# A long convolution's transforms taken at odd half frequencies, with its matmuls in groups of four banks

## The reference

```python
# hyena: v, x1, x0 are short convolutions (width 3) of the projection
z = v * x1
# h_fwd, h_bwd: 256 taps each, from a small MLP with sine activations times a decay
# y[t] = sum_{s<=t} h_fwd[t-s] z[s] + sum_{s>t} h_bwd[s-t] z[s]   (two-sided, per channel)
y = (longconv(z, h_fwd, h_bwd) + hy_skip * z) * x0
```

## Time and profile before

| | |
|---|---|
| median of three executions | 2644.22 us |
| the profiled execution's own time | 2645.37 us |
| its span, first to last instruction | 2643.6 us |
| granted PE clock, mean | 0.998 |
| PE, DVE, ACT, POOL busy | 2626.3, 1931.1, 1509.1, 387.5 us |
| PE matmuls in float32 of `fkm`, `zfm`, `zim` (records; two make a matmul) | 40, 32, 48 |

### The profile page before, as it was taken

One profiled execution on the slowest core, in us unless ns is written; L12 is line 12 of the kernel. 1 busy time (PEld: TensorE's weight loads), 2 busy tenths in 40 slices (PEclk: granted clock), 3 DMA queues, 4 the chain that ended last, 5 costly groups with the idle time before them and its releaser, 6 DMA issues.

```text
span 2643.6 us, 38894 instructions
## 1 busy us (share of the span) xinstructions
PE 2626.3 (99%) x15146; PEld 2279.0 (86%) x15146; DVE 1931.1 (73%) x2902; ACT 1509.1 (57%) x2345; POOL 387.5 (15%) x383
## 2 busy tenths in 40 slices
PE   9999999999999999999999999999999999999998
PEld 8888888888899888888888888888888888888887
DVE  7877777877967665666666698697877777777775
ACT  6655658786656444444444466545565555555555
POOL 2111003214201010000000052011101010101012
PEclk9999999999999999999999999999999999999999
DMA  7666566666656555666666666546666666666664
GB/s 238 211 190 184 176 199 188 185 197 186 201 173 196 168 159 170 189 191 187 192 188 191 191 190 220 160 128 194 188 191 186 191 190 191 189 191 188 191 184 135
DMA packets 136992, 492.89 MB, mean 186 GB/s; under 512 B 15463, under 2 KB 16552, under 8 KB 136552
## 3 DMA queue, kind: packets, MB, share of 16 engines
q1 hardware_dynamic: 136376, 489.88, 61.5%
q10 hardware_dynamic: 432, 0.52, 0.1%
HBM read 488.21 MB, written 2.13 MB: 185 GB/s over the span
## 4 chain that ended last, share of the span: by engine, by line
PE 97%; DVE 1%; ACT 1%; issue 0%; DMA 0%; SPq 0%; DVEq 0%; ACTq 0%
PE ps L871 61%; PE ps L868 30%; PE ps L885 1%; DVE wl L1443 1%; PE ps L1056 0%; DMA raw<-in_w_sc 0%; PE ps L1089 0%; PE ps L1078 0%; PE ps L1002 0%; ACT wh L1120 0%; PE ps L858 0%; PE ps L857 0%; PE ps L856 0%; PE ps L848 0%; PE ps L846 0%
## 5 line engine op out<-in xcount | busy, mean ns | idle before, releaser
L871 PE MATMUL ps<-X,wh 128*128 128x512 f32 x4848 | 1624.8, 397 | 2.6 <-DVE X L1449 2.4
L1443 DVE TENSOR_TENSOR wl<-raw,wh 128x1024 fp32r<-128x1024 f32 (+1 forms) x905 | 1178.4, 1305 | 460.2 <-ACT wh L1120 459.4
L1120 ACT ACTIVATE wh<-raw 128x1024 fp32r<-128x1024 f32 (+1 forms) x905 | 954.3, 1057 | 650.9 <-PE ps L868 612.8
L868 PE MATMUL ps<-X,wl 128*128 128x256 f32 x4848 | 1217.1, 279 | 0.0
L871 PEld LDWEIGHTS ps<-X,wh 128*128 128x128 f32 x4848 | 888.4, 188 | 196.8 <-issue 9.0
L868 PEld LDWEIGHTS ps<-X,wl 128*128 128x128 f32 x4848 | 879.7, 188 | 29.4
L871 PE MATMUL ps<-XG,wh 128*128 128x512 f32 x2176 | 730.8, 396 | 0.6 <-DVE hT L1443 0.6
L868 PE MATMUL ps<-XG,wl 128*128 128x256 f32 x2176 | 547.5, 278 | 0.0
L871 PEld LDWEIGHTS ps<-XG,wh 128*128 128x128 f32 x2176 | 395.6, 188 | 81.6 <-DVE hT L1443 1.5
L868 PEld LDWEIGHTS ps<-XG,wl 128*128 128x128 f32 x2176 | 398.3, 188 | 17.1
L1905 POOL TENSOR_TENSOR hT<-hT,T 128x256 f32<-128x256 f32 x224 | 188.3, 863 | 1426.7 <-DVE hT L1443 1426.6
(11 more groups left out here) (197 smaller groups left out, 1239.0 us busy)
## 6 DMA issues: line engine op xcount, KB each, us to landing
raw<-in_w_gate SPq DMA_DIRECT2D x176, 512.0 KB, 3.9
raw<-in_w_down SPq DMA_DIRECT2D x176, 512.0 KB, 3.8
raw<-in_w_sc SPq DMA_DIRECT2D x95, 512.0 KB, 4.2
raw<-in_w_up SPq DMA_DIRECT2D x88, 512.0 KB, 3.7
raw<-in_w_val SPq DMA_DIRECT2D x88, 512.0 KB, 3.6
raw<-in_w_zx SPq DMA_DIRECT2D x80, 512.0 KB, 4.1
raw<-in_w_in SPq DMA_DIRECT2D x68, 512.0 KB, 3.8
raw<-in_w_osc SPq DMA_DIRECT2D x32, 512.0 KB, 3.8
```

The lines of the kernel that those rows point to most:

```text
L868: t = e.matmul(bank(c, i)[:, 0:256], wl[:, b0:b0 + 128], X[:, kx * 512:kx * 512 + 256], start=False, stop=sp and kk == c.kn - 1)
L871: e.matmul(bank(c, i)[:, :], wh[:, b0:b0 + 128], X[:, kx * 512:kx * 512 + 512], start=st and kk == 0, stop=False)
L1120: return e.activation(out, in_, ACT.Copy, scale=scale)
L1443: return e.tensor_tensor(out, a, b, op)
```

## The change: what it does

The transform is taken at 256 frequencies (2k+1)/1024 instead of 257 frequencies k/512, and even and odd positions are kept apart. With E and O the sums over even and odd positions, each of the lower 128 frequencies is E+O and its mirror in the upper half E-O up to a sign, so one 128 x 128 cosine block for each of even and odd, and one sine block for each, do. `Fm` and `IF` shrink from 1024 to 512 columns.

- `fkm`: 8 single matmuls of 384 columns in two groups of four (banks 4 to 7). ACT copies the even ones, DVE then makes sum and difference straight from the odd banks (two operations each). No single frequency is left, and no `fk0`.
- `ztm`: the transposes read every second position; two steps instead of four. `zfm`: 8 single matmuls in three steps (2, 4, 2), evacuated as `fkm` is.
- a new piece `zc`: four DVE operations of 384 columns per half, before the way back.
- `zim`: per tile 4 matmuls of 128 columns; the three tiles of a half stand in one step. `zi` writes even and odd positions interleaved, read from two halves of the bank.
- `fhm` stands in two groups of four.
- All z pieces now lie between steps 563 and 582; the filter's between 294 and 309.

```diff
             for n in range(8):
-                put(s + 16 + 2 * n, "fhm", n)
-                put(s + 17 + 2 * n, "fh", n)
-            put(s + 33, "fsum", 0)
-            for n in range(10):
-                put(s + 36 + 2 * n, "fkm", n)
-                put(s + 37 + 2 * n, "fk", n)
-            put(s + 57, "fk0", 0)
+                put(s + 16 + 3 * (n // 4), "fhm", n)
+                put(s + 17 + 3 * (n // 4) + n % 4 // 2, "fh", n)
+            for st in range(2):
+                put(s + 22 + st, "fsum", st)
+            for n in range(8):
+                put(s + 26 + 3 * (n // 4), "fkm", n)
+                put(s + 27 + 3 * (n // 4) + n % 4 // 2, "fk", n)
...
+                put(e + 2 + 2 * (n // 2), "ztm", n)
+                put(e + 3 + 2 * (n // 2), "zt", n)
+            for n, d in enumerate((4, 4, 6, 6, 6, 6, 8, 8)):
+                put(e + d, "zfm", n)
+                put(e + d + (2 if n == 5 else 1), "zf", n)
+            for n, d in enumerate((9, 11, 14, 16)):
+                put(e + d, "zk", n)
+            for hf, d in ((0, 13), (1, 18)):
+                put(e + d, "zc", hf)
                 for i in range(3):
-                    put(b + 8 + i, "zim", 3 * hf + i)
-                    put(b + 9 + i, "zi", 3 * hf + i)
-                b += 12
+                    put(e + d + 1, "zim", 3 * hf + i)
+                    put(e + d + 2 + i // 2, "zi", 3 * hf + i)
...
-                    for st in range(2):
-                        t = e.matmul(b[:, 0:384], Fm[:, 512 * st + 128 * m:512 * st + 128 * m + 128],
-                                     zt[:, 768 * st + 384 * h2:768 * st + 384 * h2 + 384], start=(st == 0), stop=(st == 1))
-                    t.then_inc(zfP, 1)
+                    w.wait_ge(zA, 2 * h2 + 2)
+                    if i < 4 and m > 1:
+                        w.wait_ge(zA, 4)
+                    elif i > 3 and m % 2:
+                        w.wait_ge(zfV, m + 1)
+                    elif i > 3:
+                        w.wait_ge(zfA, m // 2 + 1)
+                    e.matmul(banks[4 + m][:, 0:384], Fm[:, 128 * m:128 * m + 128],
+                             zt[:, 768 * (m % 2) + 384 * h2:768 * (m % 2) + 384 * h2 + 384], start=True, stop=True).then_inc(zfP, 1)
...
                 if piece == "zim":
-                    w.wait_ge(zkV, 8 * h2 + 8)
+                    w.wait_ge(zkV, 12 * h2 + 12)
-                    for m in range(4):
-                        t = e.matmul(b[:, 0:256], zf[:, m, 128 * n:128 * n + 128], IF[:, 256 * m:256 * m + 256],
-                                     start=(m == 0), stop=(m == 3))
+                    for st, parts in ((0, (zf[h2][:, 0, ch], zd(h2, 1)[:, ch])), (1, (zd(h2, 0)[:, ch], zf[h2][:, 2, ch]))):
+                        for q in range(2):
+                            t = e.matmul(b[:, 128 * st:128 * st + 128], parts[q], IF[:, 256 * st + 128 * q:256 * st + 128 * q + 128],
+                                         start=(q == 0), stop=(q == 1))
...
+                if piece == "zf" and i % 2:
+                    h2, m = i // 4, i % 4
+                    z0, z1 = zf[h2][:, m - 1, :], zf[h2][:, m, :]
+                    b = banks[4 + m][:, 0:384]
+                    w.wait_ge(zfP, i + 1)
+                    w.wait_ge(zfA, i // 2 + 1)
+                    tt(z0, z1, b, ALU.add).then_inc(zfV, 1)
...
+                if piece == "zc":
+                    z = zf[i]
+                    w.wait_ge(zkV, 12 * i + 8)
+                    tt(zd(i, 0), z[:, 0, :], z[:, 1, :], ALU.subtract).then_inc(zkV, 1)
+                    tt(z[:, 0, :], z[:, 0, :], z[:, 1, :], ALU.add).then_inc(zkV, 1)
+                    tt(zd(i, 1), z[:, 2, :], z[:, 3, :], ALU.subtract).then_inc(zkV, 1)
+                    tt(z[:, 2, :], z[:, 2, :], z[:, 3, :], ALU.add).then_inc(zkV, 1)
                 if piece == "zi":
-                    stt(zT(i), zT(i), P("hy_skip", i), banks[4 + i % 2][:, 0:256], ALU.mult, ALU.add).then_inc(ziV, 1)
+                    o = zT(i).rearrange("p (s q) -> p s q", q=2)
+                    y = banks[4 + n // 2][:, 256 * (n % 2):256 * (n % 2) + 256].rearrange("p (q s) -> p s q", q=2)
+                    stt(o, o, P("hy_skip", i), y, ALU.mult, ALU.add).then_inc(ziV, 1)
```

More of the change, by code:

```diff
@@ L1048, in tensor @@
                 if piece == "fkm":
-                    m, c = i // 2, i % 2
-                    n0, n = (128 * m, 128) if m < 4 else (256, 1)
+                    c, m = i // 4, i % 4
                     w.wait_ge(fV, 27)
-                    if i > 3:
-                        w.wait_ge(fl, 2 + i - 3)
-                    for st in range(2):
[L1055 to L1058, removed]
+                    if c and m % 2:
+                        w.wait_ge(fV, 28 + m)
+                    elif c:
+                        w.wait_ge(fl, 3 + m // 2)
+                    src = (dec[:, 768 * (m % 2):768 * (m % 2) + 768], hf[:, 1536 * (m % 2):1536 * (m % 2) + 768])[m // 2]
+                    e.matmul(banks[4 + m][:, 0:384], Fm[:, 128 * m:128 * m + 128], src[:, 384 * c:384 * c + 384],
+                             start=True, stop=True).then_inc(fP, 1)
                 if piece == "ztm":
-                    st, c = i // 2, i % 2
-                    b = banks[4 + i % 2]
+                    c, st = i // 2, i % 2
                     w.wait_ge(zm, 3 * c + 3)
                     w.wait_ge(fA, 3)
-                    if i > 1:
-                        w.wait_ge(zA, i - 1)
+                    w.wait_ge(fV, 35)
+                    w.wait_ge(fl, 6)
                     for n in range(3):
-                        t = turn(b[:, 128 * n:128 * n + 128], zT(3 * c + n)[:, 128 * st:128 * st + 128])
+                        t = turn(banks[4 + i][:, 128 * n:128 * n + 128], zT(3 * c + n)[:, st::2])
                     t.then_inc(zP, 1)
@@ L1764, in vector @@
                 if piece == "fsum":
-                    w.wait_ge(fV, 22)
-                    e.memset(hf[0:1, 768:1536], 0.0).then_inc(fV, 1)
-                    for st in range(2):
-                        fw, bw = hf[:, 1536 * st:1536 * st + 768], hf[:, 1536 * st + 768:1536 * st + 1536]
-                        w.wait_ge(fV, 23)
-                        tt(dec[:, 768 * st:768 * st + 768], fw, bw, ALU.add).then_inc(fV, 1)
-                        w.wait_ge(fV, 24 + 2 * st)
-                        tt(fw, fw, bw, ALU.subtract).then_inc(fV, 1)
-                if piece == "fk" and i == 4:
-                    w.wait_ge(fl, 4)
-                    e.tensor_copy(K5[:, 4, :], K5[:, 0, :]).then_inc(fV, 1)
-                if piece == "fk0":
-                    w.wait_ge(fl, 8)
-                    e.memset(K5[0:1, 2, :], 0.0).then_inc(fV, 1)
+                    if i == 0:
+                        w.wait_ge(fV, 22)
+                        e.memset(hf[0:1, 768:1536], 0.0).then_inc(fV, 1)
+                    fw, bw = hf[:, 1536 * i:1536 * i + 768], hf[:, 1536 * i + 768:1536 * i + 1536]
+                    w.wait_ge(fV, 23)
+                    tt(dec[:, 768 * i:768 * i + 768], fw, bw, ALU.add).then_inc(fV, 1)
+                    w.wait_ge(fV, 24 + 2 * i)
+                    tt(fw, fw, bw, ALU.subtract).then_inc(fV, 1)
+                if piece == "fk" and i % 2:
+                    c, m = i // 4, i % 4
+                    k0, k1 = (KS[:, q, 384 * c:384 * c + 384] for q in (m - 1, m))
+                    b = banks[4 + m][:, 0:384]
+                    w.wait_ge(fP, 11 + i)
+                    w.wait_ge(fl, 3 + i // 2)
+                    tt(k0, k1, b, ALU.add).then_inc(fV, 1)
+                    if m == 1:
+                        tt(k1, k1, b, ALU.subtract).then_inc(fV, 1)
+                    else:
+                        tt(k1, b, k1, ALU.subtract).then_inc(fV, 1)
                 if piece == "bload":
-                    w.wait_ge(fV, 29)
-                    w.wait_ge(fl, 12)
+                    w.wait_ge(fV, 35)
+                    w.wait_ge(fl, 6)
                     e.memset(cones, 1.0).then_inc(s_cones, 1)
```

118 lines of the change are left out of this document (48 added, 70 removed).

## The result

The changed kernel takes 2627.24 us (median of 4 runs, 2626.34 to 2629.41); the kernel before took 2644.43 beside it (4 runs, 2643.92 to 2645.49). The ratio is 0.9936, between 0.9918 and 0.9953. Forecast were 2626.4 us, in a range from 2621 to 2634. The profiled execution took 2627.55 us with a span of 2625.8, which is the span that was forecast; part of that is luck, as the terms will show.

The account below looks back on a forecast made before the run. PE was taken to bound the kernel, with DVE already a second bound in z's second part. PE spared 20.5 us less 2.7 of standing gives 17.8 less: 2627.6 for the profiled execution, 2626.4 for the median, range 2621 to 2634.

Parts of the forecast that it names:

- The bound: Whole kernel: PE holds 97% of the chain, so PE time spared is saved; 20.5 us spared.
- The filter: Filter pieces on PE: 23.0 us before, 12.8 after; saved 10.2, between 8.9 and 11.7.
- z on PE: z pieces on PE: 22.3 us before, 12.0 after; saved 10.3.
- rival (c): `zim`: 128-column matmuls in a row of 12 paced by weight loads, +5.0, 2631.4 us; chance 0.08.
- `zc` and `zim` in the first part: Step 575: PE reaches `zim` after 18.0 us, DVE needs 16.8; 1.2 to spare, nothing charged.
- Rival (b): Both z parts: DVE bounds, PE waits at `zim` and the lag carries on; 2632.5 us, chance 0.13.
- What is given back: Second z part: PE runs ahead of DVE and stands 2.7 us, first before `pool1` and units behind 598.
- DVE loses 7.7: Second z part: DVE is spared 4.1 for `zk`, 0.8 for `zi`, 2.8 of slowing, against PE's 10.4.
- The rule on POOL and DVE: Second z part: by exclusion DVE could lose 2 x 2.3, giving 2624.9 us; the forecast kept slowing of 1.4 beside 2.29.
- The strided read of a bank: `zi` on DVE: alternating reads of bank halves might take twice 0.48, 1.4 later, 2628.1 us.
- (d): Six gaps waiting for evacuation or `zc`: PE's queue stops at groups; 2650.4 us at 4 us each, chance 0.04.
- (e): Whole kernel: columns not saved where they count or gain absorbed by a later wait; within 5 us of before, chance 0.06.

Follow-up runs that it names:

- grouped: The kernel before with only the eight `fhm` put in two groups of four: 2645.63 us in one run, filter stretch 148.21 for 150.90.
- one-by-one: The changed kernel with each `fhm` and `fkm` in a gap of its own: 2630.35 us, ratio 0.994, filter stretch 141.95 for 139.22.
- the kernel without waits: The changed kernel with `ln`'s end on DVE, its second half three steps later and the last two `pool1` two steps later: 2623.54 us, ratio 0.9915.

## Why the prediction was right, point by point

**The bound.** That PE's spared time is saved held: 18.5 us of stretches for 20.5 + 1.5 spared less the standing.

**The filter**, forecast 10.2, measured 11.7. The mechanism held and one term was mis-sized: `fhm`, taken as 7.5 between 6.0 and 8.8, measured 2 x 3.08 = 6.2. I took the middle of two ends where the lower was right: the grouped and the one-by-one kernels show that the extra goes with the group. `fkm` cost 2 x 2.70 = 5.4, forecast 5.3. ACT's and DVE's new work was hidden, as charged.

**z on PE**, forecast 10.3. In the kernel without waits the z stretch is 157.6, 10.7 less than before; the kernel before had some 0.5 of standing at units 599 and 604 (3.36 and 3.13 us, where some 3.23 and 2.78 are what these cost without), so PE was spared 10.2 to 10.3. The two terms that the trace before didn't show are settled. Transposes with every second position cost no more than plain ones (0.71 for six), and rival (c), pacing of 128-column matmuls by weight loads, is out: 0.225 each.

**`zc` and `zim` in the first part**, charged nothing with 1.2 to spare: held. `zim` never waited. It was thinner than counted: `zc` of step 574 ended at 1686.44 and `zim` started at 1686.87, so 0.4 were to spare. Moving POOL's products onto DVE made this `zim` 0.2 late, yet 3.4 us of extra work at step 567, eight steps ahead, still fitted. DVE was busy 49.95 of 59.2 us in this part, 0.84 where 0.87 was forecast. Rival (b), both parts bound by DVE, didn't happen, but it was the near one.

**What is given back**, forecast 2.7. Measured in the stretch 161.5 - 157.6 = 3.9 of standing, less the 0.5 of before: 3.4. The size is near, by luck: the working isn't right. I had "first before `pool1` and the units behind 598", as one sum over 67 us. The first stand is at unit 586, twelve units ahead of that, and it is a sum over 15.5 us, from 1707.81, where DVE would wait for PE's `zim`, to the end of `wl` at 1723.35. The step that failed is "DVE loses 7.7": it sets DVE's losses anywhere in the part against PE's. The products that went began at 1742.73 in the kernel before, behind unit 586, and relieve DVE only behind the first lump, while PE's loss of four `zfm` (4 x 1.32 = 5.3 us, units 583 to 586) falls into it. What I didn't look at was `ln`: POOL's half of it stayed where it was, and I counted only the POOL work that was moved away.

**The rule on POOL and DVE.** I stayed with 1.4 of slowing beside 2.29 of POOL rather than with the Trainium skill, SBUF — State Buffer, section "Who interferes with whom", by which a VectorE instruction with two SBUF inputs contends with a GpSimd instruction that reads SBUF, for a shared pair of ports that is an exclusive lock. The rows after bear the rule out: R<-R,RS and `wl`, both with two SBUF inputs, lost 3.3 us beside the 3.93 of the second `ln` on POOL. Taken one by one, the first R<-R,RS took 0.41 and the second 2.06, to 0.28 behind the end of POOL's first operation (1720.30); `wl` ended 1.09 behind the end of POOL's second (1722.27), nearly its plain 1.22. The operation with a bank as an input in the same neighbourhood took its plain 0.47 (1714.70), as the rule has it too. The 1.4 of the earlier trace rows was no case against it either: one by one, two of the four taps took 1.24 where 0.47 is plain, and each ended 0.28 behind the end of one of POOL's two operations. Short operations that start a little after POOL's and end a little after it lose less than POOL's whole time. The rule would have sent me to `ln`, where it mattered; the number that I derived from it, 2624.9, was for the wrong work, since POOL's `zk` had been moved away or hidden. It was also added up wrong: 1.8 less than 2626.4 is 2624.6, as 1.4 more (for `zi`) is 2627.8 and not 2628.1.

**The strided read of a bank.** `zi` took 0.87 for two and 0.47 for one, where the plain one took 0.48. For DVE's reads the fear drawn from the section "Door 1: The DMA port swizzle" of the same page of the Trainium skill didn't come true; of matmuls into such a bank no run here tells.

**The sum.** Forecast span 2625.8, measured 2625.8: 1.5 more saved in the filter, 0.7 more standing, and 0.9 more in the first 885 us, which is scatter. Three misses of about 1 us each cancelled, which is luck. The rivals (d), the whole queue stopping at groups, and (e), no saving, were never near: all six gaps that could wait ran without standing.

## What to carry to other kernels

Where one engine bounds and another is nearly full, don't set the two busy times of a long stretch against each other. Look for the lumps: from the point where the second engine last waited, count its work up to the operation that the first waits for, and compare that with the first engine's work over the same units; what lies outside a lump can be taken away or added without effect, as long as the second engine has room there. This is shown for the stand at unit 586; for the one at `pool1` only that it goes when the piece is moved. A change that takes work from the bounding engine shortens its side of every such comparison, so the lumps to look at are those that it did not touch. A long stand can cost more than itself: 4.6 us of it took 3.1 more at the lower clock. And where a small matrix piece has a fixed extra, put its pieces side by side; where it has none, as `fkm` here, grouping wins nothing.

## What the runs showed of the hardware

- A float32 matmul with 64 rows costs 1.10 us alone and 3.08 for four in a row, so some 0.5 us is paid once per group; with 128 rows it is 0.66 alone and 2.70 for four, nothing extra. No run changed the number of rows and nothing else, so that the rows are the cause is likely and not shown.
- Operations with two inputs in SBUF on DVE can double in time beside POOL's (`wl` 2.42 and 2.85 for 1.22). It also goes the other way: POOL's first product of `zk`, begun at 1686.58, took 3.46 us where the one behind it took 1.39, while `wl` and the two products behind it on DVE took their plain times to 1689.18. Timelines of DVE and POOL in the changed kernel:

```profile
1687.03 1.21 DVE L1440 TENSOR_TENSOR wl<-raw,wh 128x1024 fp32r<-128x1024 f32 x1
...
1686.58 3.46 POOL L1926 TENSOR_TENSOR Gf<-A 128x384 f32<-128x384 f32 x1 [9.24 <-DVE Gf L1440]
1690.12 1.39 POOL L1926 TENSOR_TENSOR A<-A 128x384 f32<-128x384 f32 x1
```

- So giving POOL work can be worse for DVE than doing it there: with 1.5 us more of its own for each `ln`, DVE was ready earlier.
- PE's granted clock fell to 0.50 (1.2 GHz) after it had stood for some 4 us, and matmuls of 128 columns then took 0.44 us instead of 0.225 each.
- The first 885 us of one and the same work differ by up to 5.4 us between the twelve traces. Up to 4.9 of it arises in the first 47 us. Another 1.5 arises between 615 and 637 us: these units take 18.8 us in four traces and 20.3 to 20.5 in the other eight, and those eight alone have 3.4 us at a granted clock of 0.50 there. Why some executions have it and others not stays open; no run was made for it.
